# One ring of weight columns under the projections of the normed tokens, loaded and split for the next while the last pair is multiplied

## What is computed

```python
h = rms_norm(x, norm_w[l]) * (1.0 + scale[:, None, :]) + shift[:, None, :]
parts = split_in(h @ w_in[l])
q = mla_q(parts[0], ...)
k, v = mla_kv(parts[1], parts[2], ...)
attn = attend(q, ...)
y = mixer_branches(parts, attn, ...)
x_new = x + gate[:, None, :] * (y @ w_out[l])
```

## Time and profile before

| | |
|---|---|
| median of 3 runs | 4788.84 us (4785.28 to 4797.52) |
| the profiled execution | 4786.71 us, span of its records 4784.9 us |
| PE busy | 4007.2 us, 84% of the span |
| weight loads of PE | 2896.3 us, 61% |
| DVE busy | 2177.8 us, 46% |
| ACT busy | 1473.1 us, 31% |
| POOL busy | 905.0 us, 19% |
| mean granted clock of PE | 0.914 of 2.4 GHz |

### The profile page before, as it was taken

How to read it: one execution, slowest core, us unless ns; L and a number is a source line. 1 busy time by engine, 2 the same in 40 slices (tenths; PEclk the granted TensorE clock), 3 DMA queues, 4 the chain that set the end, 5 groups by cost and what they waited for, 6 DMA issues and landing times. The chain is left out here.

```text
span 4784.9 us, 43684 instructions
## 1 busy us (share of the span) xinstructions
PE 4007.2 (84%) x16492; PEld 2896.3 (61%) x16492; DVE 2177.8 (46%) x2598; ACT 1473.1 (31%) x2342; POOL 905.0 (19%) x414
## 2 busy tenths in 40 slices
PE   6699779997689689998585989898999755999996
PEld 6578535556567445556363866576777644666664
DVE  0274356662355356641346623233442212666665
ACT  1211235551201144440214135412221011555552
POOL 0143210001143400003130102133333331111111
PEclk9899879997899889998798999999999985999998
DMA  4111101101211101212221212043343231999986
GB/s 156 60 36 32 34 15 31 31 27 49 80 44 38 42 27 53 64 60 99 30 31 53 49 33 26 11 72 75 80 97 70 63 136 52 345 350 352 353 293 224
DMA packets 354883, 450.97 MB, mean 94 GB/s; under 512 B 51997, under 2 KB 227314, under 8 KB 354178
## 3 DMA queue, kind: packets, MB, share of 16 engines
q1 hardware_dynamic: 342034, 423.12, 29.9%
q0 software_dynamic: 12656, 25.26, 1.5%
HBM read 408.41 MB, written 59.31 MB: 98 GB/s over the span
## 5 line engine op out<-in xcount | busy, mean ns | idle before, releaser
L1076 PE MATMUL values<-probs,vp 128*128 128x512 f32 x672 | 348.9, 601 | 12.0 <-issue 6.4
L1165 ACT ACTIVATE probs<-scores 128x512 f32<-128x512 f32 (+1 forms) x336 | 196.1, 584 | 309.2 <-PE scores L211 307.5
L1374 POOL TENSOR_TENSOR out_hi<-out_w,ones 128x1024 fp32r<-128x1024 f32 x24 | 57.3, 2387 | 1196.9 <-DMA out_w<-in_w_out 1196.9
L209 PE MATMUL scores<-q_hi,k_rest 97*128 97x512 f32 (+1 forms) x336 | 262.4, 781 | 0.0
L678 DVE SCALAR_TENSOR_TENSOR conv_out<-conv_in,vectors,conv_out 128x1295 f32<-128x1295 f32 (+1 forms) x120 | 254.2, 2118 | 4.3
L3258 PE MATMUL dp<-h_t,abt 128*128 128x512 f32 x544 | 241.9, 597 | 1.1 <-ACT abt L3307 0.9
L209 PE MATMUL out_ps<-h_t_r,out_w_r 128*128 128x512 f32 (+1 forms) x448 | 172.6, 385 | 68.0 <-POOL out_w_r L1376 68.0
L209 PE MATMUL gates_ps<-x_t_r,gates_w_r 128*128 128x512 f32 (+1 forms) x560 | 210.3, 375 | 21.9 <-POOL gates_w_r L259 21.9
L3289 ACT ACTIVATE expert_hi<-wu 128x1024 fp32r<-128x1024 f32 x136 | 144.9, 1065 | 252.1 <-PE gp L211 252.1
L1247 DVE TENSOR_REDUCE mx<-made 128x1 f32<-128x640 f32 (+1 forms) x272 | 203.8, 794 | 27.0 <-PE made L1017 26.4
L209 PE MATMUL smb<-x_t_r,merge_w_r 128*128 128x512 f32 x480 | 196.3, 409 | 19.3 <-POOL merge_w_r L2599 16.6
(11 more groups left out here) (523 smaller groups left out, 9872.9 us busy)
## 6 DMA issues: line engine op xcount, KB each, us to landing
wg<-in_w_gate SPq DMA_DIRECT2D x34, 2048.0 KB, 9.9
wu<-in_w_up SPq DMA_DIRECT2D x34, 2048.0 KB, 11.2
h_t<-in_w_down SPq DMA_DIRECT2D x34, 2048.0 KB, 9.8
ahead_w<-in_w_ada SPq DMA_DIRECT2D x48, 512.0 KB, 3.9
gates_w<-in_w_in SPq DMA_DIRECT2D x28, 512.0 KB, 3.9
mod_w<-in_w_mod SPq DMA_DIRECT2D x12, 1024.0 KB, 5.5
x_kept<-x_t SPq DMA_DIRECT2D x6, 2048.0 KB, 11.0
ahead_w<-in_w_mod SPq DMA_DIRECT2D x24, 512.0 KB, 3.5
```

Of the source, the lines that this page charges most:

```text
L209: nc.tensor.matmul(out, lhs[1], rhs[0], start=start, stop=False, **kw)
L1076: nc.tensor.matmul(O[b % 2][:, 0:w], vp[g // 2 % 2][:, kb, g % 2 * VD:g % 2 * VD + P], pr[m % 3][:, 0:w], start=kb == 0, stop=kb == nk - 1 ...
L1165: nc.scalar.activation(pr[m % 3][:, 0:w], S[m % 2][:, 0:w], ACT.Exp, scale=scale).then_inc(s.exped, 1)
L1374: nc.gpsimd.tensor_tensor(hi[:, c, :, :], wt[:, c, :, :], all_ones(k), ALU.mult).then_inc(s.split, 1)
```

## The change

A ring of one pair of weight columns lives through stages 1 to 6 of a layer, with semaphores of its own, at the right end of SBUF. `load_half` loads the half with the running number n, `split_half` splits it:

```diff
+@contextmanager
+def weight_ring(nc, name):
+    with ExitStack() as es:
+        s = es.enter_context(stage(nc, "ring_in0 ring_in1 ring_split"))
+        w = es.enter_context(nc.sbuf_tensor(f"{name}_w_{nc.next_id()}", [P, 2, DK, P], F32, side="right"))
+        rest = nc.alloc_sbuf_tensor_at(f"{name}_r_{nc.next_id()}", [P, 2, DK, P], F32R, offset=nc.sbuf_top)
+        hi = es.enter_context(nc.sbuf_tensor(f"{name}_hi_{nc.next_id()}", [P, 2, DK, P], F32R, side="right"))
+        yield named(w=w, rest=rest, hi=hi, w_in=(s.ring_in0, s.ring_in1), split=s.ring_split, pairs=0, halves=0)
+def load_half(sp, ring, n, columns):
+    c = n % 2
+    sp.dma_start(ring.w[:, c, :, :], columns[:, :, c * P:(c + 1) * P]).then_inc(ring.w_in[c], 16)
+def split_half(nc, k, ring, pool, n):
+    c = n % 2
+    pool.wait_ge(ring.w_in[c], 16 * (n // 2) + 16)
+    nc.gpsimd.tensor_tensor(ring.hi[:, c, :, :], ring.w[:, c, :, :], all_ones(k), ALU.mult).then_inc(ring.split, 1)
+    pool.wait_ge(ring.split, 2 * n + 1)
+    nc.gpsimd.tensor_tensor(ring.rest[:, c, :, :], ring.w[:, c, :, :], ring.hi[:, c, :, :].bitcast(F32), ALU.subtract)\
+        .then_inc(ring.split, 1)
```

`ring_gemm` takes the place of `split_gemm` in the three projections. It differs in that its own first pair is expected to be loaded, and that at its end it loads the pair of the next projection, `then`, each half when PE is done with the half before it; it splits the first of the two, and leaves the second to the next stage:

```diff
+    first, split_before = ring.pairs, ring.halves
+    split_here = 2 * (first + n_pairs) + (1 if then is not None else 0)
...
+            if then is not None:
+                for c in range(2):
+                    sp.wait_ge(s.products, (n_pairs - 1) * per + (c + 1) * nb)
+                    load_half(sp, ring, 2 * (first + n_pairs) + c, then)
...
+            for n in range(split_before, split_here):
+                split_half(nc, k, ring, pool, n)
```

The very first pair is loaded and split in the norm. There POOL also clears three stretches of 15 columns at the convolution's edges, and the stage that cleared all of it is gone:

```diff
+                if ring:
+                    for n in range(2):
+                        load_half(sp, ring, n, columns)
                 for i, (t0, w, _) in enumerate(blocks):
                     sp.dma_start(kept[:, :, t0:t0 + w], src[:, :, t0:t0 + w]).then_inc(s.all[i], 16)
...
+        if ring:
+            @block.gpsimd
+            def _(pool):
+                for n in range(2):
+                    split_half(nc, k, ring, pool, n)
+                ring.halves = 2
+                for edge in edges:
+                    nc.gpsimd.memset(edge, 0.0).then_inc(s.cleared, 1)
...
-        with stage(nc, "cleared") as s, nc.Block() as block:
-            @block.gpsimd
-            def _(pool):
-                nc.gpsimd.memset(u[:, :, :], 0.0).then_inc(s.cleared, 1)
...
+            @block.gpsimd
+            def _(pool):
+                split_half(nc, k, ring, pool, ring.halves)
+                ring.halves += 1
```

More of the change, by code:

```diff
@@ new lines, in ring_gemm, with walk, _, load @@
+def ring_gemm(nc, k, name, ring, parts, blocks, then=None, extra=None):
+    nb = len(blocks)
+    per = 2 * nb
+    n_pairs = sum(part[0] for part in parts)
+    first, split_before = ring.pairs, ring.halves
+    split_here = 2 * (first + n_pairs) + (1 if then is not None else 0)
+    names = "products evacuated " + (extra[0] if extra else "")
+    with ExitStack() as es, stage(nc, names) as s, nc.Block() as block:
+        ps = [es.enter_context(psum(nc, f"{name}_ps{t}", [P, 512], F32)) for t in range(per)]
+        def walk(eng, step):
+            over_pairs(eng, parts, 2, step, True)
+        @block.sync
+        def _(sp):
+            def load(g, slot, part, p, turn):
+                for c in range(2):
+                    if g:
+                        sp.wait_ge(s.products, (g - 1) * per + (c + 1) * nb)
+                        load_half(sp, ring, 2 * (first + g) + c, part[1](p))
+            walk(sp, load)
+            if then is not None:
+                for c in range(2):
+                    sp.wait_ge(s.products, (n_pairs - 1) * per + (c + 1) * nb)
[4 more added lines that the diff above has]
+                split_half(nc, k, ring, pool, n)
+        @block.tensor
+        def _(pe):
+            def products(g, slot, part, p, turn):
+                for c in range(2):
+                    pe.wait_ge(ring.split, 4 * (first + g) + 2 * c + 2)
+                    for b in range(nb):
+                        t = c * nb + b
+                        t0, width, _ = blocks[b]
+                        if g:
+                            pe.wait_ge(s.evacuated, (g - 1) * per + t + 1)
+                        for j in range(DK):
+                            last = split_matmul(nc, ps[t][:, 0:width], (ring.hi[:, c, j, :], ring.rest[:, c, j, :]),
+                                                split_h(k, j, t0, width), start=j == 0, stop=j == DK - 1)
+                        last.then_inc(s.products, 1)
+            walk(pe, products)
+        @block.scalar
+        def _(act):
+            def evacuate(g, slot, part, p, turn):
+                for c in range(2):
+                    for b in range(nb):
+                        t = c * nb + b
+                        act.wait_ge(s.products, g * per + t + 1)
+                        part[2](p, c, b, ps[t][:, 0:blocks[b][1]], slot).then_inc(s.evacuated, 1)
+            walk(act, evacuate)
+        if extra:
+            extra[1](block, s, walk, lambda eng, sem, value: eng.sem_inc(sem, value))
+    ring.pairs, ring.halves = first + n_pairs, split_here
@@ L629, in short_branch, with conv_branches @@
     return program
[L632 removed]
+def conv_branches(nc, k, l, w_in, cf_pw, blocks, u, sc, ring):
     w_ids = [w for _, w, _ in blocks]
```

44 lines of the change are left out of this document (26 added, 18 removed).

## The result

| | before | after |
|---|---|---|
| median, us | 4790.7 (4785.28 to 4797.52, 4 runs) | 4709.29 (4701.2 to 4711.66, 4 runs) |
| ratio, with its 95% interval | 1 | 0.9826 [0.9809, 0.9844] |
| profiled execution, us | 4786.7 | 4711.66 |
| its span, us | 4784.9 | 4709.8 |
| mean granted clock of TensorE | 0.914 | 0.907 |

The change takes 81.4 us off the median of these runs, 1.7%. The forecast of 4717 was 7.7 us too high.

What follows compares the result with a forecast made beforehand. The prediction took these stages to be bound by PE's wait for load and split plus PE's work. 64.3 + 8.0 - 0.7 = 71.6 us off 4786.7 gave 4715.1, forecast as a 4717 median; range 4706 to 4734.

Steps and rivals of the forecast that it cites:

- The wait at each start: At the six starts of cf, gates and latents, PE no longer waits for load and split: 64.28 us gained.
- The clock: Gates and latents start at full instead of half clock: 8.0 us gained, bounds 0 and 8.7; nothing before cf.
- rival B: At gates and latents the clock stays low after sparse PE work in the layer norm: 8.0 lost, 4725; chance 0.09.
- The barrier: Behind the latents, clearing the ring's semaphores with one more barrier per layer costs 0.7 us for two.
- What is added: Prefetch loads and splits beside cf's end, gates' first half, layer norm and norm: each taken as costing 0.
- rival D: In the projections, late loads or splits make PE wait in each half, slower than before: 4803; chance 0.02.
- rival A: In the layer norm, DVE's centring is held by the split after all: 2 x 4.1 us lost, 4725; chance 0.12.
- the later stores: In the norm, two loads issued ahead of the stores of x: taken as 0, at most 3.4 us a layer.
- Rival C: The norm grows by splits holding DVE or by late stores: 16.6 or 6.8 us lost, 4734 or 4724; chance 0.08.
- PE's wait plus PE's work: The length of the cf, gates and latents stages: each microsecond off the wait is one off the span.
- The time below which I would have misread the stages: A median below 4700 us (or above 4740) would mean misreading what these stages wait for.
- E: A start still waits for load or split; gates and latents keep 39.3 and 8.0 us, 4764 left; chance 0.04.

Runs made afterwards that it cites:

- Run 1: Changed kernel, but gates and latents load and split their first pair when their stage starts; only cf's is prefetched in the norm: 4756.35 us.
- Run 5: Kernel before, with 40 useless matmuls at the start of each gates and latents stage, filling the wait: 4783.84 us, ratio 0.9987.
- run 7: Changed kernel, with twenty useless matmuls behind the norm's sums, in both layers: 4703.67 us.
- run 3: Kernel before, with unused gaps putting the weights of cf and gates at 480 modulo 512 bytes: 4781.24 us, ratio 0.9975.
- run 8: Changed kernel, with gaps giving the later projections' weights and operands the tokens' remainder modulo 512 bytes: 4697.28 us.
- Run 6: Changed kernel, with the norm's splits delayed on POOL until DVE has begun scaling the third block: 4727.26 us.
- run 2: Changed kernel, with the ring moved by 384 bytes so its weights lie at 96 modulo 512: 4723.85 us.

## Why the prediction was right, and where it was not

**The wait at each start: right.** The groups give 64.1 for the 64.28 forecast; term by term 24.8, 19.3 and 20.0 for 24.96, 19.40 and 19.92. PE's remaining idle times are 18.07, 1.27 and 1.44, as named beforehand. Run 1 confirms the division in time, 47.1 for gates and latents against 47.3.

**The clock: right in the mechanism and, by the traces, in size.** Gates and latents start at 1.00, so rival B falls. Run 5 gave 7.9 by the lengths of its stages, and 5.4 with an interval of 1 to 11 by its times, for the forecast 8.0. Cf got nothing, as said, since 18 us of idle time remain before it; run 7 is what that costs, 5.6 by the medians and 4.5 by the lengths of cf.

**The barrier: right, 0.64 for 0.7.** From the start of the latents' last product to the start of the next stage's first product PE takes 3.38 us in both layers before the change and 3.70 in both after it, 0.32 more each time. The other traces agree: 3.37 to 3.47 in the two further ones of the kernel before (runs 3 and 5), 3.70 to 3.80 in all with the ring. What is between is the closing of the ring, the clearing and the barrier together.

**What is added: right, and the absorbed cost was real.** The second half of the gates' first pair is split from 257.49, beside PE's first half, and PE's idle time before the gates is 2.6 in all, so the lane isn't late (rival D). The centring was not held: rival A falls by these rows, DVE and POOL in the layer norm of layer 0:
```profile
451.76 1.29 DVE L873 SCALAR_TENSOR_TENSOR conv_out<-mean,conv_out 128x512 f32<-128x512 f32 x2 [0.96 <-PE mean L827]
453.48 1.29 DVE L873 SCALAR_TENSOR_TENSOR conv_out<-mean,conv_out 128x512 f32<-128x512 f32 x2 [0.43 <-PE mean L827]
...
451.79 2.36 POOL L245 TENSOR_TENSOR ring_hi<-ring_w,ones 128x1024 fp32r<-128x1024 f32 x1 [8.91 <-DMA ring_w<-in_w_in]
```

Both pairs of instructions took 1.29, 0.65 each, with the first split beside one pair and the end of it and the start of the next beside the other. The norm's end did not move by more than it moves without a cause. From ACT's first square to DVE's last instruction it takes 48.65 us in layer 0 instead of 47.50, and 47.5 in layer 1 in both kernels; but runs 3 and 5, with the old norm, have 48.1 and 47.0 in layer 0, and runs 7 and 8, with the new one, 46.9 and 46.6. So no cost of the later stores shows. Rival C's mechanism took 3.55 and 4.21 us from DVE, and the idle time behind took it in. Run 6 shows the price where the cover is gone, 18 us, close to the 16.6 that the prediction had worked out for that case.

**The term that was missing, in "PE's wait plus PE's work".** The prediction took PE's work as given and only its clock as open. The means of 366 ns for the latents and 375 for the gates stood in the earlier trace rows, but they mix two shapes, and the step from one matmul of 512 columns to the next was not compared between stages. The change moved the weights to another place, and that by itself was worth 10.8 us in run 3 (14.6 in run 2, where the latents got slower too). The sum with it is 64.1 + 8.0 + 10.8 - 0.6 = 82.3 against 81.4 of the medians. Without it the forecast was 7.7 too high. That it stayed in its range was luck in this one respect, since the range had been drawn for errors of other kinds.

**The rivals.** E, that a start would keep its wait, falls by the groups. D falls by the absence of idle time in the middle of the stages. The time below which I would have misread the stages, 4700, wasn't reached, but a term of 10 us was missing all the same.

## What to carry to other kernels

Where PE waits for a chain of load and split at each stage start, the idle time of the first matmul in the stage, less the idle time that the stage change leaves, is what a prefetch across the boundary gives; add what the clock then keeps. When a change moves buffers, compare the step between two matmuls in the middle of a stage, at equal clock, before anything else: two stages of one form that differ in it are a hint that needs no change to be seen. Before speeding PE up in a stage, look how often PE waits inside it for the weights' lane: the deltanet and the state space model, with 5 and 7 such waits in 157 and 152 us, gave nothing that stood out, while the merge, with 6 in 487, gave 6.2 us.

## What the runs showed of the hardware

In the middle of a stage at a granted clock of 1.00, the step between two float32r matmuls of 512 columns was 0.227 us where weights and streamed tokens lie at the same remainder modulo 512 bytes. It was 0.233 to 0.234 where the remainders were 32, 96, 128 or 192 bytes apart (counted round the 512). This held for either of the two being moved, and in every projection that was lined up, the state space model's included. The deltanet's gate, 192 bytes apart, had 0.229 in most traces and 0.233 in run 1, at the same addresses; lined up it had 0.227. It was tried with this form alone, not finely between these distances, and not at 256.

A DVE instruction with both inputs in SBUF was held 1.8 to 2.1 us by each split of 2.35 to 2.8 us on POOL, and one with an input in PSUM (0.65) not at all. PE standing idle for 1.3 us kept the clock at 1.00, and the first matmuls of cf behind 18 us were at 0.50 for 5.2 us; useless matmuls in place of the wait kept it at 1.00. Clearing the ring's three semaphores and one more barrier cost 0.32 us between two stages. One load was split 13.4 us after its issue in one trace and 11.2 in another, against 6.8 to 7.8 in the other nine of eleven, and PE waited for it.
